# Sample attention in six units, keys loaded before values, and uneven shares of wide matmuls in linear attention

## The reference, cut to what matters

```python
h = x + 0.5 * SwiGLU_1(RMSNorm(x))
q_a, k_a, v_a, r_a, f_a, q_b, k_b, v_b, g_a, g_b = split(RMSNorm(h) @ w_in)
# A: gated linear attention, 4 heads (key 128, value 256), state S_t = diag(a_t) S_{t-1} + k_t^T v_t
o_a = rmsnorm_per_head(q_dec @ S_before + causal(q_dec @ k_inv^T) @ v) * silu(r_a)
# B: band attention, 16 heads of 64: a chunk of 64 frames sees itself and the 8 chunks before it
o_b = softmax(q k^T / 8 + bias[clip(q_pos - k_pos, -128, 128)]) @ v
h = h + (sigmoid(g_a) * (o_a @ w_branch_gla) + sigmoid(g_b) * (o_b @ w_branch_att)) @ w_out
y = RMSNorm(h + 0.5 * SwiGLU_2(RMSNorm(h)))
```

## Time and profile before

| | |
|---|---|
| median of 3 runs | 3776.93 us (3775.7 to 3779.49) |
| profiled execution, its own time | 3780.06 us |
| span of its slowest core (core 1) | 3778.5 us |
| spans of the eight cores | 3759.6 to 3778.5 us |
| PE busy | 3583.7 us, 95% |
| DVE busy | 1403.7 us, 37% |
| ACT busy | 1226.5 us, 32% |
| POOL busy | 408.1 us, 11% |

### The profile page before, as it was taken

How to read it: one execution, slowest core, us unless ns; L and a number is a source line. 1 busy time by engine, 2 the same in 40 slices (tenths; PEclk the granted TensorE clock), 3 DMA queues, 4 the chain that set the end, 5 groups by cost and what they waited for, 6 DMA issues and landing times.

```text
span 3778.5 us, 60686 instructions; the slowest of 8 cores (3759.6 to 3778.5 us)
## 1 busy us (share of the span) xinstructions
PE 3583.7 (95%) x20944; PEld 1695.9 (45%) x20944; DVE 1403.7 (37%) x2384; ACT 1226.5 (32%) x2287; POOL 408.1 (11%) x920
## 2 busy tenths in 40 slices
PE   7999999999989999998778999999989999999998
PEld 4444444444444444444443444444444444444444
DVE  2222222222364654546244545463642222222222
ACT  2112211122343635445234354452632221222221
POOL 1032222221000000011100000011010000000000
PEclk9999999999999999999779999999999999999999
DMA  9687777768324343352953433425273121012110
GB/s 184 138 161 154 161 157 164 158 138 207 119 94 157 106 152 123 123 171 85 250 179 116 145 133 112 168 79 180 91 268 110 51 67 62 34 57 67 54 48 26
DMA packets 118505, 477.04 MB, mean 126 GB/s; under 512 B 21999, under 2 KB 22784, under 8 KB 88896
## 3 DMA queue, kind: packets, MB, share of 16 engines
q1 hardware_dynamic: 60096, 330.22, 27.0%
q0 software_dynamic: 58112, 142.95, 17.7%
HBM read 430.96 MB, written 101.97 MB: 141 GB/s over the span
## 4 chain that ended last, share of the span: by engine, by line
PE 85%; DVE 6%; DMA 3%; issue 3%; ACT 2%; POOL 1%; DVEq 0%; SPq 0%; ACTq 0%; POOLq 0%
PE ps L383 79%; PE ps L1083 2%; PE ps L1038 2%; PE ps L454 1%; DVE s_op L1095 1%; DMA s_wring<-wsc 1%; DVE s_va L981 1%; DMA s_nr<-hB 1%; DMA s_vone<-cv 1%; DVE s_oa L1260 1%; ACT s_tmpa L1047 1%; DVE s_oaT L461 1%; DVE s_Sf L1223 1%; DVE s_Pb L1062 0%; PE ps L1107 0%
## 5 line engine op out<-in xcount | busy, mean ns | idle before, releaser
L383 PE MATMUL ps<-s_xnT,s_wring 128*128 128x512 bf16 (+1 forms) x2880 | 629.7, 364 | 31.4 <-DMA s_wring<-wsc 7.8
L383 PE MATMUL ps<-s_xnT,s_w1b 128*128 128x512 bf16 x2816 | 614.1, 380 | 0.0
L383 PE MATMUL ps<-s_xnT,s_w2b 128*128 128x512 bf16 x2816 | 612.5, 379 | 0.0
L647 ACT ACTIVATE s_tmpf<-ps 128x512 f32<-128x512 f32 x352 | 209.4, 595 | 1194.9 <-PE ps L383 1194.8
L649 DVE TENSOR_TENSOR s_gT<-ps,s_tmpf 128x512 bf16<-128x512 f32 x352 | 243.5, 692 | 948.8 <-PE ps L383 870.9
L383 PE MATMUL ps<-s_wring,s_xnT 128*128 128x512 bf16 (+1 forms) x1728 | 408.6, 387 | 34.0 <-DVE s_va L981 19.0
L383 PEld LDWEIGHTS ps<-s_xnT,s_w1b 128*128 128x128 bf16 x2816 | 274.4, 98 | 328.5 <-issue 2.5
L383 PEld LDWEIGHTS ps<-s_xnT,s_w2b 128*128 128x128 bf16 x2816 | 274.1, 98 | 327.4
L383 PEld LDWEIGHTS ps<-s_xnT,s_wring 128*128 128x128 bf16 x2880 | 252.0, 100 | 319.9 <-issue 75.5
L383 PE MATMUL ps<-s_w1c,s_gT 128*128 128x512 bf16 x1408 | 312.1, 380 | 0.0
L383 PE MATMUL ps<-s_w2c,s_gT 128*128 128x512 bf16 x1408 | 310.1, 379 | 0.0
(11 more groups left out here) (137 smaller groups left out, 3139.7 us busy)
## 6 DMA issues: line engine op xcount, KB each, us to landing
s_wring<-wsc SPq DMA_DIRECT2D x198, 1024.0 KB, 5.9
s_stg<-wms POOLq DMA_DIRECT2D x88, 256.0 KB, 5.8
wsc<-s_stg POOLq DMA_DIRECT2D x88, 256.0 KB, 4.4
s_stg<-w2s POOLq DMA_DIRECT2D x66, 256.0 KB, 5.9
w2b<-s_stg POOLq DMA_DIRECT2D x66, 256.0 KB, 4.4
s_rring<-xp SPq DMA_DIRECT2D x32, 512.0 KB, 10.8
hA<-s_rring SPq DMA_DIRECT2D x32, 512.0 KB, 8.1
s_hb<-hA SPq DMA_DIRECT2D x8, 2048.0 KB, 12.8
```

The source lines that it names most:

```text
L383: ins = e.matmul(out_ap, lhsT=l, rhs=r, start=(start and i == 0), stop=(stop and i == n - 1))
L647: S.op("act", (lambda e, b=bg_, tb=tb, T=T: e.activation(out=tmpf[:, tb, 0:T], in_=bank(b)[:, 0:T], func=AF.Silu)), reads=[("ps", bg_)], w ...
```

## The change

Three things change.

(1) `cache_load` issues the four key transfers first and then the eight of the values, in the same order as before.

(2) In the sample tile a unit of attention covers several head pairs. For each half of the head pairs (c0 = 0, 4) there is one unit with the sample's own keys (r = 4) for four head pairs, and two units, each with the four cached blocks for two head pairs: six units instead of 16. Scores, factors, products with the values and transposes are the same matmuls and factors; the exponentials, reciprocals, scalings and copies out of PSUM act on up to four head pairs at once. The stream is fed 81 over these units instead of 130 over the 16. Prompt tiles keep their units and amounts.

(3) In `gla` of a prompt tile, the steps are no longer alike: a step of the last row block, from output 3 on (`late`), feeds 50/6 = 8.33, any other 78/17 = 4.59. Before, each fed 128/22 = 5.82. The sample tile keeps 128/7.

The diff, cut to its core:

```diff
             for blk in range(4):
                 S.op("pool", (lambda e, blk=blk: e.dma_start(out=ckst[:, blk, :], in_=ck[blk * 128:(blk + 1) * 128, :])),
                      writes=[("ckst", blk)], dma=True)
+            for blk in range(4):
                 for hp in range(2):
                     S.op("pool", (lambda e, blk=blk, hp=hp: e.dma_start(
                         out=vone[:, blk, :, hp * 128:hp * 128 + 64],
...
             if kind == "s":
-                groups = [[(4, 0)], [(3, 0), (0, 1), (1, 2), (2, 3)]]
+                NI, R = 4, 3
+                units = []
+                for c0 in (0, 4):
+                    units.append([(c0 + i, 4, i) for i in range(4)])
+                    for c1 in (c0, c0 + 2):
+                        units.append([(c1 + i, 3, i) for i in range(2)] + [(c1 + i, r, 2 + 3 * i + r) for i in range(2) for r in range(3)])
...
-            units = [(c, g) for c in range(8) for g in range(len(groups))]
+                R = len(groups)
+                units = [[(c, r, c0) for r, c0 in g] for c in range(8) for g in groups]
...
-                    for s in subs:
-                        ins = e.transpose(out=pb_[:, s * 128:s * 128 + TP], in_=op[:TP, s, :], identity=identb[:TP, :TP])
+                    for i in range(NI):
+                        ins = e.transpose(out=pb_[:, i * 128:i * 128 + TP], in_=op[:TP, i, :], identity=identb[:TP, :TP])
...
+                    S.op("dve", lambda e: e.tensor_copy(out=obT[:, 4 * c:4 * c + 4, 0:TP],
+                                                        in_=pb_.rearrange("p (k t) -> p k t", k=8)[:, 0:4, 0:TP]),
+                         reads=[("ps", b)], writes=[("qbT", 4 * c + i, 0) for i in range(4)])
...
-            step_ = 130.0 / (2 * len(units))
+            step_ = (130.0 if kind == "p" else 81.0) / (2 * len(units))
...
-                    yield
+                    yield late if s == NS - 1 else 1
                     sc = 32 + 8 * (s % 2)
...
                     root(TP, sc, 4, 4.0 / 256, 4.0 * EPS)
-                    yield
-                    yield
+                    yield late if s == NS - 1 else 1
+                    yield late if s == NS - 1 else 1
...
                             reads=[("ps", bo[hh // 2]), ("gst", sc + 4 + hh), ("rr", s, hh // 2)], writes=[("oa", s, hh)])
-                    yield
+                    yield late if s == NS - 1 else 1
...
                         transpose_sub(oa[:TP, s - 1, :], TP, oaT, s - 1, 3, [("oa", s - 1, hh) for hh in range(4)], ("oaT", s - 1), pool="G")
-                        yield
-                yield
+                        yield late if s == NS - 1 else 1
+                yield late
...
-            woven(gla(), stream, 128.0 / (5 * NS + 2))
+            step_ = 128.0 / (5 * NS + 2)
+            late = 1.0
+            if NS > 1:
+                step_, late = 78.0 / (5 * NS - 3), 50.0 / 6 * (5 * NS - 3) / 78.0
+            woven(gla(), stream, step_)
```

More of the change, by code:

```diff
@@ L1025, in keyrows, with stagebuf @@
                 return TP if r == 4 else 128
+            def stagebuf(u):
+                return tmpa[:, u % 2, :, :], ("tmpa", u % 2)
             def att_sc(u):
-                c, g = units[u]
-                pbuf, tb = u % NB, u % 2
+                pbuf = u % NB
+                ta, tkey = stagebuf(u)
                 b = ps_alloc("Q")
@@ L1033, in fns @@
                     ins = None
-                    for r, c0 in groups[g]:
+                    for c, r, c0 in units[u]:
                         s0, n, _ = span(r)
@@ L1040, in fns @@
                     return ins
-                S.op("pe", fns, reads=[("qbT", c, s) for s in subs] + [("kbT", keyslot(r), c) for r, _ in groups[g]],
+                S.op("pe", fns, reads=[("qbT", c, s) for c, _, _ in units[u] for s in subs] + [("kbT", keyslot(r), c) for c, r, _ in units[u]],
                      writes=[("ps", b), ("ps", b + 1)])
-                nk = keyrows(groups[g][0][0])
-                nb = sum(span(r)[2] for r, _ in groups[g])
-                n = sum(span(r)[1] for r, _ in groups[g])
+                nk = keyrows(units[u][0][1])
+                nb = sum(span(r)[2] for _, r, _ in units[u])
+                n = sum(span(r)[1] for _, r, _ in units[u])
                 if nb:
-                    S.op("act", lambda e: e.activation(out=tmpa[:nk, tb, :, 0:nb * TP], in_=ps[:nk, b:b + 2, 0:nb * TP], func=AF.Exp, scale=0.125),
-                         reads=[("ps", b), ("ps", b + 1)], writes=[("tmpa", tb)])
+                    S.op("act", lambda e: e.activation(out=ta[:nk, :, 0:nb * TP], in_=ps[:nk, b:b + 2, 0:nb * TP], func=AF.Exp, scale=0.125),
+                         reads=[("ps", b), ("ps", b + 1)], writes=[tkey])
                 if n > nb:
@@ L1071, in att_pv @@
             def att_pv(u):
-                c, g = units[u]
                 pbuf = u % NB
-                begins, ends_ = g == 0, g == len(groups) - 1
+                begins, ends_ = u % R == 0, u % R == R - 1
                 def fnv(e):
@@ L1078, in fnv @@
                     for hp in range(2):
-                        for i, (r, c0) in enumerate(groups[g]):
-                            s0, n, _ = span(r)
+                        todo = [(c, r, c0 + s - s0, s, s if kind == "p" else c % 4) for c, r, c0 in units[u] for s0 in (span(r)[0],)
+                                for s in range(s0, s0 + span(r)[1])]
+                        for i, (c, r, b0, s, o_) in enumerate(todo):
                             nk, sl = keyrows(r), keyslot(r)
-                            for s in range(s0, s0 + n):
-                                ins = e.matmul(bank(6 + hp)[:TP, s * 65:s * 65 + 65], lhsT=Pb[:nk, pbuf, hp, (c0 + s - s0) * TP:(c0 + s - s0 + 1) * TP],
-                                               rhs=vone[:nk, sl, c, hp * 127:hp * 127 + 65], start=(begins and s == 0),
-                                               stop=(ends_ and i == len(groups[g]) - 1 and s == s0 + n - 1))
+                            ins = e.matmul(bank(6 + hp)[:TP, o_ * 65:o_ * 65 + 65], lhsT=Pb[:nk, pbuf, hp, b0 * TP:(b0 + 1) * TP],
+                                           rhs=vone[:nk, sl, c, hp * 127:hp * 127 + 65], start=(begins and i == 0),
+                                           stop=(ends_ and i == len(todo) - 1))
                     return ins
-                S.op("pe", fnv, reads=[("Pb", pbuf, 0), ("Pb", pbuf, 1), "vone1"] + [("vone", keyslot(r), c // 4) for r, _ in groups[g]],
+                S.op("pe", fnv, reads=[("Pb", pbuf, 0), ("Pb", pbuf, 1), "vone1"] + [("vone", keyslot(r), c // 4) for c, r, _ in units[u]],
                      writes=[("ps", 6), ("ps", 7)])
@@ L1105, in fn @@
                     ins = None
[L1106 to L1107 removed]
+                    for i in range(NI):
+                        ins = e.transpose(out=pb_[:, i * 128:i * 128 + TP], in_=op[:TP, i, :], identity=identb[:TP, :TP])
                     return ins
                 S.op("pe", fn, reads=[("op", 0), ("op", 1), "identb"], writes=[("ps", b)])
[L1110 to L1111 removed]
+                if kind == "p":
+                    S.op("dve", lambda e: e.tensor_copy(out=obT[:, c, 0:T], in_=pb_[:, 0:T]),
+                         reads=[("ps", b)], writes=[("qbT", c, s) for s in subs])
+                else:
+                    S.op("dve", lambda e: e.tensor_copy(out=obT[:, 4 * c:4 * c + 4, 0:TP],
+                                                        in_=pb_.rearrange("p (k t) -> p k t", k=8)[:, 0:4, 0:TP]),
+                         reads=[("ps", b)], writes=[("qbT", 4 * c + i, 0) for i in range(4)])
             DEPTH = 2
[L1114 removed]
             def attention():
```

26 lines of the change are left out of this document (12 added, 14 removed).

## The result

The changed kernel is slower. Over executions of both kernels on the same chip the ratio of its time to that of the kernel before is 1.0084, with a 95% interval of 1.0071 to 1.0098. On the 3776.93 us of before that is 3808.7 us; the forecast of 3806 was a ratio of 1.0077. The medians of all executions (3811.18 us against 3826.15) can't be set side by side, because in some executions the clock of one die falls and the time grows by several per cent; those, and in one profile the four cores of that die, are left out here.

A forecast was written before the change was run, and what follows sets the result against it. In prompt-tile linear attention, PE's matmul stream and the DVE/ACT chain were taken as almost exactly balanced. Late weighting +38.4, keys first -2.5 and six units -6.5 make +29.4 us: 3809.5, or 3806 against the median, range 3783 to 3826.

The forecast's parts named there:

- part 2: Cached loads, keys issued before values: PE's 4.65 us wait for key load 4 goes; -2.5 us, bounds 0 and 4.65.
- The total: Sum over the profiled execution's 3780.06 us: +38.4 - 2.5 - 6.5 = +29.4, so 3809.5, or 3806 against the median.
- Part 1: Prompt-tile linear attention, late weighting: queue order on DVE and ACT makes PE stall; +4.8 us a tile, +38.4, bounds +15 and +46.
- the firm bound: Prompt-tile linear attention: product 4 waits for mixT of product 3, not before 2104.8; at least +1.9 us a tile.
- The balance of the two sides: Linear attention rounds of rows 0 to 2: vector chain 9.43 us from oa to oa, PE 9.7 us, almost exactly balanced.
- the two gaps that the change was to close: End of linear attention: 0.75 us before the last transposes, about 0.4 of 1.76 before the first oaT product; 1.15 a tile.
- Part 3: Sample attention in six units: fewer, larger vector operations, 3 to 4 us idle staying; -6.5 us, bounds 3 and 9.
- Only the firm bound (3783): Prompt tiles: inserted mixT and tanh operations cost nothing, only +1.9 us a tile; 3783, chance 0.12.
- Slack in rows 0 to 2 (3759): Prompt tiles: PE really gets 4.3 us ahead before output 3, late work fills gaps, -1.15 a tile; 3759, chance 0.10.
- Falls of the clock in the prompt tiles (3820): Prompt tiles: new 2.5 us stalls bring the clock down briefly, up to 14 us in eight tiles; 3820, chance 0.08.
- That the change doesn't shorten the sample tile (3815): Sample tile not shortened at all because the store's landing decides; 3815, inside the main forecast's range, no chance of its own.
- The sample tile at the upper level (3794): Sample tile: denser attention is granted 2.4 GHz, some 12 us less; 3794, chance 0.08.

The follow-up runs named there:

- even steps: Changed kernel with every linear attention step feeding 128/22 again, keys first and six units kept; ratio 0.9975 (0.9932 to 1.0018).
- the early tanh: Changed kernel with even steps and only the gate's tanh written right behind its second piece of matmuls, mixT left as before; 3811.41 us.
- 8 moved matmuls: Changed kernel with steps of 92/18 ahead of output 3 and 36/6 from it on, 8 wide matmuls moved instead of 20; 3789.52 us in one execution.

## Where the prediction failed, and where it held

**The step that failed** is in part 2, keys first, which puts the price of the loads' new order at nothing: "The hidden price of the move, the values landing later, is covered: they are first read after 1877", with "the values' chain, which still ends near 1838.58". Forecast: -2.5 us with bounds of 0 and -4.65. Measured alone, in the sample stretch: +3.0 in the first run; in the second, on four cores, +5.1 against the mean of before and +2.2 against the same four cores of before (156.7). All are outside the bounds. The first reader of the values isn't what matters. On POOL's queue the stores of hB and then the kept rows stand behind the values' chain, and `Pb` waits for them. I named that queue and left it out of the sum. On core 1 of before, from which the wait for the keys was priced, the stores already landed late, so little was left to lose there; five of the eight cores had no such wait to win back. With six units the price is hidden by the ring, and part 2 comes to between -2.0 and +0.4 us (mean 147.5 against 149.4 and 147.1).

**The total** came out close by luck in its terms: +29.4 us forecast against the profiled execution, 30.05 measured (3810.11 - 3780.06). The sample stretch was to lose 9.0 us and lost 5.0. The six merges, which the sum doesn't have, gave back 4.2, and the rest of the span took 3.6 more.

**Part 1, the late weighting: right in mechanism and size.** Forecast +38.4, measured +37.8 in the stages; the run with this part alone gives the whole loss. Two of its sums are a little off: the firm bound comes to 2122.73 - 2120.62 = 2.1 us a tile, not 1.9, and the terms behind output 3 add up to 45.4, not 45.3. The balance of the two sides was read from one round; oa to oa in that tile of before is 8.69, 9.43 and 8.12 us. The times that were followed, against the tile at 2522.63 (from state 0): oa of row 0 9.65, measured 9.64; Sf 2 12.2 (12.20); squares 1 15.4 (15.22); oa of row 1 19.2 to 21.2 (19.00 to 21.05); mixT of product 3 ending 25.5 (25.33); the wait behind it 2.5 (2.38); oa of row 2 28.7 (28.41); the first oaT product 45.3 (44.96). The wait of product 5 for mixT, forecast at 1.4, isn't in this tile, because the fall of the clock takes its place; where the clock stays up it is 1.44. Gate 4 waited 1.15 for its tanh, which I had put among the smaller waits. Of the two gaps that the change was to close, the one of 0.75 went, and 0.28 of the other where 0.4 was forecast.

**Part 3, six units: right.** Forecast -6.5 (-3 to -9). From the sample stretches of the kernels with 16 units and the old order of loads (153.8 and 154.5) to those with six (147.1 and 149.4) it is -5.9; attention itself is 8 us shorter. What I had wrong is what limits it: 3 to 4 us of idle time were to stay for the finishes, but what stays is the weight ring.

**The rivals.** Only the firm bound (3783): excluded by 45.05 us a stage, where it would have given 42.2. Slack in rows 0 to 2 (3759): excluded, as oa to oa is 9.36, 9.41 and 9.72 us in after, against 8.69, 9.43 and 8.12 before; none is below 8.0. Falls of the clock in the prompt tiles (3820): they came, behind the wait of 2.38 us in 45 of 64 stages, but its price didn't: with the fall a stage takes 45.03 us, without 45.10, since PE had to wait for mixT next in any case. PE's busy time over the span doesn't show them, because the merges and the sample stretch spend less time at the lower level than before. That the change doesn't shorten the sample tile (3815): excluded by the 5.0 us. The sample tile at the upper level (3794): a small part came true, below.

## What to carry to other kernels

Where each engine takes its work in one fixed order, feeding filler by another schedule doesn't only move the filler: it moves the small operations that close each filler group against those of the dependent chain. Before moving any, write down for each vector queue what stands ahead of the chain's operations, and whether that itself waits for something; 0.6 us of foreign work, or 0.7 us of foreign waiting, per round is what a balanced loop can't give back. A gap at the end of a stage can cost more than its length where the clock falls behind it. For a reordered load, follow its queue to the last store behind it and to who waits for that, and read the rows on several cores before a wait is priced.

## What the runs showed of the hardware

**Clock.** In sample attention the granted clock rose from a mean of 0.67 over the cores to 0.73 in after and 0.75 in after with even steps, while sample linear attention stayed at 0.50 to 0.52. Windows of after, core 1, in which attention runs from 1877.1 to 1904.4:

```profile
1877.00:1880.50 3.50, 2.04 (x69) 1.69 (x68) 1.88 (x5) 1.46 (x3) 0.59 (x2) 1.00 1.03 272
1880.50:1886.50 6.00, 0.41 (x18) 0.23 (x9) 0.17 (x1) 0.19 (x1) 0.00 (x0) 0.86 0.94 270
1886.50:1890.00 3.50, 1.87 (x30) 1.59 (x31) 2.15 (x10) 1.81 (x3) 0.00 (x0) 0.50 1.03 421
1890.00:1894.00 4.00, 4.00 (x69) 3.53 (x70) 1.78 (x7) 1.87 (x4) 0.00 (x0) 0.50 0.95 395
1894.00:1898.00 4.00, 3.29 (x30) 1.58 (x29) 2.28 (x8) 1.77 (x4) 0.00 (x0) 0.87 0.86 256
1898.00:1904.40 6.40, 4.58 (x73) 2.97 (x70) 2.64 (x10) 0.22 (x1) 0.00 (x0) 1.00 0.86 279
```

PE is at 2.4 GHz until it has nothing to do for most of 6 us, comes back at 1.2 GHz (0.50), works there without a gap for 4 us, and is back at 1.00 by 1898. The Trainium skill, TensorE: Matmul & The Clock Gate, section "Why this matters for your kernels", gives a long idle gap as the cause of half rate; here, with a gap of 7.2 us in the list of waits, the trace agrees; in the prompt stages of after it fell behind waits of 2.38 us. In the 16-unit attention of before the clock was down with waits for op of 1.1 us at most. The prediction took that as a fall without a long gap, but on core 1 such a gap stands just ahead of the window that it read, and the clock fell at 1873.3, inside it:

```profile
1877.75 0.28 PE L1083 MATMUL ps<-s_vone,s_Pb 64*64 64x65 bf16 x2 [5.42 <-DVE s_Pb L1062]
```

On core 5 of before, though, the clock fell at 1865.5 with no wait over 1.5 us in the ten us before, so a long gap isn't the only cause. A mean of 0.73 is 46 per cent of the time at the upper level (0.67 is 34), and the 268 matmuls of sample attention kept PE busy for 17.1 us on average where it was 22.5: how much of that is the clock and how much the denser order wasn't separated.

**A load behind four others.** In before POOL waited 4.0 to 9.8 us on the eight cores for the first load of half a block of cached values, which stood behind one key load. Behind four it waited 9.8 to 16.9 us in the two runs of keys first alone (8 and 4 cores) and 10.1 to 16.5 in after. Here "at once" for the keys meant "later" for the values.

**The clock behind short waits.** In linear attention and the merges of the prompt tiles PE is at 1.00 but for short falls. The falls to 0.50 stand behind one wait of 2.38 us (45 of 64 stages of after) or behind two waits with eight transposes between them (0.75 and 1.76 us in before: 21 of 48 merges; 2.74 and 1.65 with the early tanh: 48 of 48). A fall costs time only where PE isn't about to wait anyway: 1.6 us for each of the 21.

**What stays open.** It isn't shown why the transfers behind the values take longer with keys first, nor why 8 moved matmuls cost more for each than 4 or 20. The best version that was run is the kernel before with the six units alone, 0.9984 (0.9974 to 0.9994); the changed kernel with even steps is as good within the noise, 0.9975 (0.9932 to 1.0018).
